# A branch on TensorE put behind four weight units, attention scores in pairs of heads, and key sums put ahead of row maxima

## The reference, cut to what matters

```python
def mla_mixer(...):
    ...
    q = rmsnorm(q, q_norm)                    # 8 heads of 128 + 64
    k = rmsnorm(k, k_norm)
    ...
    for blk in range(seq // Q_BLOCK):         # two blocks of 128 queries
        ...
        scores = jnp.einsum('bqhd,bkhd->bhqk', q[:, s0:end], k[:, :end]).astype(jnp.float32) * scale
        mask = jnp.arange(end)[None, :] <= (s0 + jnp.arange(Q_BLOCK))[:, None]
        p = jax.nn.softmax(jnp.where(mask, scores, neg), axis=-1).astype(v.dtype)
        outs.append(jnp.einsum('bhqk,bkhd->bqhd', p, v[:, :end]))

def moe_swiglu(h, router, w_gate, w_up, w_down):
    ...
    for e in range(N_EXPERTS):
        out = out + gates[:, e:e + 1] * swiglu(ht, w_gate[e], w_up[e], w_down[e])
```

## Time and profile before

| | us |
|---|---|
| median of three runs | 1259.41 |
| the profiled execution's own time | 1259.81 |
| its span, first to last instruction | 1257.9 |
| PE matmul busy | 1233.1 (98%) |
| DVE busy | 998.4 (79%) |
| ACT busy | 844.0 (67%) |

### The profile page before, as it was taken

One profiled execution on the slowest core, in us unless ns is written; L12 is line 12 of the kernel. 1 busy time (PEld: TensorE's weight loads), 2 busy tenths in 40 slices (PEclk: granted clock), 3 DMA queues, 4 the chain that ended last, 5 costly groups with the idle time before them and its releaser, 6 DMA issues.

```text
span 1257.9 us, 18129 instructions
## 1 busy us (share of the span) xinstructions
PE 1233.1 (98%) x5924; PEld 1015.4 (81%) x5924; DVE 998.4 (79%) x1397; ACT 844.0 (67%) x1218; POOL 40.0 (3%) x47
## 2 busy tenths in 40 slices
PE   7999999999999999999999999999999999999998
PEld 6888888888778788888888888888886877888887
DVE  5687555556876899999999999999999887765664
ACT  6566444446755788888888888888886686644443
POOL 0000000000100000000000000000100121000000
PEclk9999999999999999999999999999999999999999
DMA  9735545554233699999999999999997632455540
GB/s 365 293 126 225 196 173 191 177 196 168 70 134 133 246 379 372 383 344 367 371 396 366 362 374 365 392 350 364 370 421 281 245 146 101 168 184 185 184 150 34
DMA packets 48388, 325.41 MB, mean 259 GB/s; under 512 B 5512, under 2 KB 6672, under 8 KB 10192
## 3 DMA queue, kind: packets, MB, share of 16 engines
q1 hardware_dynamic: 44896, 316.59, 66.7%
q10 hardware_dynamic: 2752, 5.77, 1.2%
q0 software_dynamic: 688, 2.36, 0.5%
HBM read 318.93 MB, written 5.77 MB: 258 GB/s over the span
## 4 chain that ended last, share of the span: by engine, by line
PE 91%; DVE 4%; ACT 2%; issue 1%; DMA 1%; POOL 0%; SPq 0%; DVEq 0%; ACTq 0%
PE bank L434 26%; PE bank L436 26%; PE bank L435 25%; PE bank L1141 4%; PE bank L1142 2%; PE bank L498 2%; DVE wl L1834 1%; PE bank L848 1%; ACT wh L1202 1%; PE bank L703 1%; PE bank L470 1%; PE bank L1140 1%; DMA x<-x_dram 1%; PE bank L702 1%; DVE xt L1854 0%
## 5 line engine op out<-in xcount | busy, mean ns | idle before, releaser
L1834 DVE TENSOR_TENSOR wl<-raw,wh 128x1024 fp32r<-128x1024 f32 x598 | 712.7, 1219 | 171.0 <-ACT wh L1202 161.1
L1202 ACT ACTIVATE wh<-raw 128x1024 fp32r<-128x1024 f32 x598 | 630.3, 1058 | 266.6 <-PE bank L436 224.7
L434 PE MATMUL bank<-wh,xt 128*128 128x512 f32 (+2 forms) x1026 | 407.1, 397 | 5.7 <-DVE xt L1854 2.6
L436 PE MATMUL bank<-wh,xt 128*128 128x512 f32 (+2 forms) x1026 | 398.0, 388 | 0.0
L435 PE MATMUL bank<-wl,xt 128*128 128x512 f32 (+2 forms) x1026 | 397.3, 387 | 0.0
L434 PEld LDWEIGHTS bank<-wh,xt 128*128 128x128 f32 x1026 | 193.6, 189 | 44.7 <-DVE xt L1854 3.2
L436 PEld LDWEIGHTS bank<-wh,xt 128*128 128x128 f32 x1026 | 193.3, 188 | 40.3
L435 PEld LDWEIGHTS bank<-wl,xt 128*128 128x128 f32 x1026 | 194.0, 189 | 36.2
L434 PE MATMUL bank<-wh,hth 128*128 128x512 f32 x472 | 185.2, 392 | 0.1
L436 PE MATMUL bank<-wh,htl 128*128 128x512 f32 x472 | 184.1, 390 | 0.0
L435 PE MATMUL bank<-wl,hth 128*128 128x512 f32 x472 | 183.8, 389 | 0.0
(11 more groups left out here) (304 smaller groups left out, 809.2 us busy)
## 6 DMA issues: line engine op xcount, KB each, us to landing
raw<-weights_dram SPq DMA_DIRECT2D x298, 1024.0 KB, 6.5
expert_results<-wide ACTq DMA_DIRECT2D x7, 512.0 KB
x<-x_dram SPq DMA_DIRECT2D x2, 512.0 KB, 5.4
raw<-weights_dram SPq DMA_DIRECT2D x2, 512.0 KB, 7.4
wide<-bias_scratch ACTq DMA_DIRECT2D x8, 128.0 KB, 6.4
out_dram<-x SPq DMA_DIRECT2D x4, 256.0 KB, 2.0
fixed<-fixed_dram SPq DMA_DIRECT2D x1, 536.0 KB, 17.3
bias_scratch<-act ACTq DMA_DIRECT2D x2, 256.0 KB, 5.2
```

Source lines behind the costliest of these rows:

```text
L434: mm(o, lh, wh[:, wi, sl], start=start, stop=False)
L436: return mm(o, ll, wh[:, wi, sl], start=False, stop=stop)
L1202: A(wh[:, c % SPLIT, 0:n], raw[:, (c // 2) % RAW, (c % 2) * UNIT:(c % 2) * UNIT + n], ACT.Copy).then_inc(hi_done, 1)
L1834: V.tensor_tensor(wl[:, c % SPLIT, 0:n], raw[:, (c // 2) % RAW, (c % 2) * UNIT:(c % 2) * UNIT + n], f32(wh[:, c % SPLIT, 0:n]), ALU.subtra ...
```

## The change

- PE's branch for crowded experts becomes a function `crowd`, which runs behind the first four units of expert 0 instead of ahead of them. The load of the flag stays where it is. Inside the branch bank 1 takes the place of bank 0, on PE, ACT and DVE.
- Heads 0 and 1, and heads 4 and 5, get their scores by `scores_pair`: for each query block the 128-row products of both heads, then the 64-row products of both heads, which lie on different rows and in different banks. Heads 2, 3, 6 and 7 stay as they are.
- `k_sums(1)` goes ahead of `row_max(0)` on DVE.

```diff
             def ffn(tag, c0, nf, U, loops, width, nd, i0, f0=0, nt=NT, early=None, late=None, done=0, rows_ready=None,
-                    second=None, last_turn=None, first=False, half=0):
+                    second=None, last_turn=None, first=False, half=0, behind=None):
...
                     up(c0, i0, rows_ready)
                     if early:
                         early()
+                    if behind:
+                        behind()
                     up(c0 + ug, i0, None, bank[6:7], after={1: lambda: turn(0, fb)})
...
+            def scores_pair(h):
+
+                places = ((0, P), (P, 2 * P))
+                if h >= 2:
+                    pe.wait_ge(sem("head_nm"), h)
+                for qb, (a, n) in enumerate(places):
+                    for s in (h, h + 1):
+                        mm(bank[4 + s % 2][:, a:a + n], qnT[:, s, qb * P:(qb + 1) * P], knT[:, s, 0:n], start=True, stop=False)
+                    for s in (h, h + 1):
+                        r0 = (s % 2) * 64
+                        last = mm(bank[4 + s % 2][:, a:a + n], qrT[r0:r0 + 64, s // 2, qb * P:(qb + 1) * P],
+                                  krT[r0:r0 + 64, s // 2, 0:n], start=False, stop=True)
+                        if qb == 1:
+                            last.then_inc(sem("head_S"), 1)
...
-            scores(0)
-            scores(1)
+            scores_pair(0)
             pe.wait_ge(sem("v_c"), 2)
...
-            scores(4)
-            scores(5)
+            scores_pair(4)
             wo(0)
...
             crowded = pe.value_load(order[0:1, 9:10], min_val=0, max_val=1)
-            with pe.If(crowded > 0):
+
+            def crowd():
+
+                with pe.If(crowded > 0):
...
-            expert(0, 0, 2, first=True)
+            expert(0, 0, 2, first=True, behind=crowd)
...
             q_scales(0)
+            k_sums(1)
             row_max(0)
-            k_sums(1)
             row_max(1)
```

More of the change, by code:

```diff
@@ L886, in _ @@
             crowded = pe.value_load(order[0:1, 9:10], min_val=0, max_val=1)
-            with pe.If(crowded > 0):
[L888 to L909, removed]
-                            for n in range(2):
[L911 to L920, removed]
@@ new lines, in crowd @@
+            def crowd():
+                with pe.If(crowded > 0):
+                    pe.wait_ge(sem("moe_gl"), KD)
+                    pe.wait_ge(sem("order"), 2)
+                    passes = pe.value_load(order[0:1, 8:9], min_val=0, max_val=MORE)
+                    with pe.Fori(0, passes) as v:
+                        gather_rest(v)
+                        for t in range(NT):
+                            last = nc.tensor.transpose(bank[3][:, t * P:(t + 1) * P], osel[:, t, :], ident)
+                        last.then_inc(sem("o_selT"), 1)
+                        pe.wait_ge(sem("o_xt"), v * 2 + 2)
+                        for f in range(8):
+                            pe.wait_ge(sem("o_up"), v * 256 + 32 * (f + 1))
+                            for k in range(KD):
+                                last = mm(bank[1][:, :], oxt[:, k, :], opanel[:, k // 4, (k % 4) * WIDE:(k % 4 + 1) * WIDE],
+                                          start=(k == 0), stop=(k == KD - 1))
+                            last.then_inc(sem("o_gu"), 1)
+                            pe.wait_ge(sem("o_h"), v * 8 + f + 1)
+                            for j in range(2):
+                                last = nc.tensor.transpose(bank[2][:, j * P:(j + 1) * P], hbuf[:, 0, j * P:(j + 1) * P], ident)
+                            last.then_inc(sem("o_hT"), 1)
+                            pe.wait_ge(sem("o_hc"), v * 8 + f + 1)
+                            pe.wait_ge(sem("o_down"), v * 128 + 16 * (f + 1))
+                            for j in range(2):
+                                for n in range(2):
+                                    last = mm(bank[4 + n][:, :], oht[:, j, :],
+                                              opanel[:, 2, j * D + n * WIDE:j * D + (n + 1) * WIDE],
+                                              start=(f == 0 and j == 0), stop=(f == 7 and j == 1))
+                            last.then_inc(sem("o_d"), 1)
+                        pe.wait_ge(sem("o_y"), v * 2 + 2)
+                        for t in range(NT):
+                            for n in range(2):
+                                mm(bank[(2, 3, 1, 4)[2 * t + n]][:, :], oselt[:, t * P:(t + 1) * P],
+                                   oy[:, n * WIDE:(n + 1) * WIDE], start=True, stop=True).then_inc(sem("o_S"), 1)
+                        pe.wait_ge(sem("o_x"), v * 4 + 4)
@@ L1598, in _ @@
                         sc.wait_ge(sem("o_gu"), v * 8 + f + 1)
-                        A(ebuf[:, 0, 0:FG], bank[0][:, 0:FG], ACT.Tanh, scale=0.5).then_inc(sem("o_e"), 1)
+                        A(ebuf[:, 0, 0:FG], bank[1][:, 0:FG], ACT.Tanh, scale=0.5).then_inc(sem("o_e"), 1)
                         sc.wait_ge(sem("o_hT"), v * 8 + f + 1)
@@ L2494, in _ @@
                     for f in range(8):
-                        g, u, h = bank[0][:, 0:FG], bank[0][:, FG:2 * FG], hbuf[:, 0, 0:FG]
+                        g, u, h = bank[1][:, 0:FG], bank[1][:, FG:2 * FG], hbuf[:, 0, 0:FG]
                         dv.wait_ge(sem("o_e"), v * 8 + f + 1)
```

## The result

The changed kernel takes 1253.08 us in the median of five runs (1252.34 to 1255.49), beside 1259.86 for the kernel before: a ratio of 0.995 [0.9939, 0.9961], 6.8 us. Three more comparisons gave 0.9945 [0.9931, 0.9958], 0.9942 [0.9929, 0.9956] and 0.9952 [0.9939, 0.9965], or 6.6, 6.9 and 5.3 us. The profiled execution took 1252.34 us, with a span of 1250.4.

A forecast was written before the change was run, and what follows sets the result against it. TensorE (PE), holding 91% of the span, was taken to bound the kernel. Branch 2.1, first pair 0.85 and second pair 1.35 summed to 4.3 us, for a median of 1255.1 us, range 1253.6 to 1257.9.

The forecast's parts named there:

- gap ahead of the expert, removed: Before the first expert's unit 0: PE's idle time is its branch, and moving the branch saves 2.1 us.
- left over behind the fourth unit: After unit 3 of the first expert: PE's queue hides the moved 3.583 us branch except for 0 to 0.15 us.
- first pair, to the turning of head 0: Scores of heads 0 and 1: pairing saves 1.44 us, of which 0.85 arrives, between 0.4 and 1.4.
- second pair, to the turning of head 4: Scores of heads 4 and 5: pairing saves 1.44 us, of which 1.35 arrives, between 0.7 and 1.45.
- rival 1: First expert: ScalarE and VectorE are held behind their own branches; total gain 2.5 to 3.4 us, chance 0.12.
- rival 3: Paired scores: halves run one after the other, or weights come later; 0.9 us less gain, 1256.0 us, chance 0.10.
- Key sums ahead: VectorE before the first maximum: costs nothing under the later scores; without them, about a microsecond of delay.
- the cover: Behind unit 3: PE's queue runs 16 to 18 pairs ahead, covering 3.6 to 4.1 us of the branch.
- rival 2: Head of the expert gains nothing: VectorE release, or 2.1 us of branch open behind unit 3; 1257.2 us, chance 0.14.
- The step that failed: Whole kernel: gains are subtracted from the profiled execution of 1259.81 us, with the median taken 0.4 us lower.
- the addition of 0.7 for scatter: Range: 0.7 us added on either side because the runs shown spread 2.4 us, giving 1253.6 to 1257.9.
- rival 4: Moved branch: its target is fetched behind weight panels and the clock may fall; 3.9 us slower, 1263.3 us, chance 0.05.

The follow-up runs named there:

- the short body: Loop of passes left out of PE's branch for crowded experts: in the kernel before 1255.88 us (0.9972), in the changed kernel 1253.95 us (0.9945).
- the maximum first: Changed kernel with the first head's maximum put back ahead of the key sums on VectorE: 1255.51 us, 0.9963 of the kernel before.
- the shortened body: Changed kernel with the skipped branch body's eight panel steps written as one, a loop of six, and one: 1252.69 us, 0.9941 of the kernel before.
- the branch part alone: Kernel before with only the branch moved behind four units, scores and key sums as before: 1257.89 us, 0.9982 of the kernel before.
- the scores part alone: Kernel before with only the paired scores and the key sums first, the branch where it was: 1257.01 us, 0.9968 of the kernel before.
- the first pair and the branch: Changed kernel with heads 4 and 5 scored one after the other again: 1256.56 us, 0.997 of the kernel before.
- the shortened body and four pairs: Changed kernel with panel steps as one, a loop of six, and one, and heads 2, 3 and 6, 7 also paired: 1254.19 us, 0.9954 of before.
- the second experiment: Four kernels beside the kernel before (1259.60 us): changed with heads 4 and 5 unpaired, changed with maximum before key sums, before and changed without the branch's loop.
- the kernel before with more products: Kernel before with seven instead of three idle-filling products on TensorE ahead of the first gather: 1259.73 us, 0.9999 of the kernel before.
- A later arrival by 1.6 us: Changed kernel with ten idle-filling products ahead of the last turning of the first attention: 1256.12 us, 0.9967 of the kernel before.
- the four-pair kernel: Changed kernel with heads 2 and 3, and 6 and 7, scored in pairs too: 1253.67 us, 0.9953 of the kernel before.

## Why the prediction was wrong, although its terms held

**The terms.** At their own places, in traces:

| term | forecast us | measured us |
|---|---|---|
| gap ahead of the expert, removed | 2.1 | 2.26 |
| left over behind the fourth unit | 0 to 0.15 | 0.06 to 0.44 |
| first pair, to the turning of head 0 | 0.85 | 1.12 |
| second pair, to the turning of head 4 | 1.35 | 1.45 |
| sum | 4.3 | 4.4 to 4.8 |

The branch is what the gap was, as the earlier trace rows had it: shown by the short body. ACT and DVE moved with PE (0.61 and 0.79 us idle ahead of their first splits, for a forecast of 0.8 to 1.0), so rival 1 is out. The pairs take 2.65 and 2.73 us for a forecast of 2.60 to 2.63, so the halves run at the price of one, and rival 3 is out. Key sums ahead "cost nothing" because the later scores hide them; with the maximum first 0.71 us are gone, which the prediction had not priced (its microsecond is for key sums ahead without the pair's later scores). The one term that was a little off is the cover: "16 to 18 of them are 3.6 to 4.1 us", of which 0.15 go to the first load, and 3.40 were measured against a branch that varies from 3.44 to 3.86 us from trace to trace. So the gap of rival 2 behind the fourth unit is there, at a fifth of its price or less. The first pair came out 0.3 better than "between 0.4 and 1.4, I take 0.85", since nothing up to head 3 took back what it gave.

**The step that failed** is the first of the sum: "The sum is made against the profiled execution, 1259.81 us ... the median of the runs shown is 0.4 lower", and with it the addition of 0.7 for scatter at the end. It takes the stretches at 1.2 GHz of the kernel before as a fixed part of both kernels. They are not. Of 68 runs of the kernel before one has a mean granted clock of 0.999 or more, of 20 of the changed kernel 11. A line with one slope for both kernels, laid through these 88 runs against the mean clock, gives 0.65 us for each thousandth of clock and 5.5 us (standard error 0.2) between the kernels at equal clock; the mean clocks, 0.9967 and 0.9982, are worth another 1.0. Together that is the 6.5 us between the means. So of the 2.2 us that the forecast missed, 1.0 is clock and 0.1 to 0.5 the terms; the 0.7 to 1.1 that are left between 4.4 to 4.8 in the traces and 5.5 by the line are found in part only. The line counts a stretch at 1.2 GHz the same wherever it falls, and the traces don't. The kernel before and the changed kernel with the shortened body have two such stretches each in their traces, in router and gather and where the second attention begins. From the first score to the end they are 5.1 us apart (925.5 and 920.4), and 0.7 of that is the gather: the stretch costs 1.5 us where it begins with the gather, as in the kernel before, and 0.8 where it begins 2 us ahead of it, because there it first lengthens idle-filling products into a wait. That is one pair of traces, so the failed step accounts for 1.0 us by the line and for 1.7 perhaps; the rest stays open. The mean clock alone can't hold it: the 33 runs of the kernel before and the 5 of the changed one that both have 0.997 are 6.2 us apart in their means. The start of an execution scatters by more than what is left: in traces of the same changed kernel the first score comes at 331.36 and at 332.83 (above).

The prediction had the pieces. It quoted the clock of 0.69 in the gather, and in rival 4 priced a stretch at 1.2 GHz at 1.7 us, but only as a loss that the change might bring. That the same stretches are losses of the kernel before that the change might remove, since it takes out 2 us in which PE stands idle, was not asked. One such stretch taken off the low end, 1.7, would have put it at 1251.9 and the measured time inside.

**Why the clock is better** is settled in part only. Neither part alone gives it: the branch part alone has 0.999 or more in 1 of 11 runs, the scores part alone in 1 of 10, the first pair and the branch in 1 of 7, the kernel before with its gap closed by the short body in 0 of 9. But the whole change doesn't always keep it: with the maximum first it is 0 of 5, with the short body 1 of 5, with the shortened body and four pairs 1 of 5, beside 11 of 20 as it is. The short body takes one more wait out of PE's way, so less idle time alone doesn't make a better clock. The four kernels of the second experiment ran on one chip, and the changed kernel did not run on it, so that their clocks can't be told from the chip's; the kernel before had no lower clock there than elsewhere (0.9972 in the mean, 0.9964 to 0.9967 on the three others).

The 18 traces say where. A stretch at 1.2 GHz in router or gather stands in all 7 of kernels without the whole change and in 6 of the 11 with it (the one with the maximum first among them); one where the second attention begins in 3 of the 7 and 5 of the 11. So by this count, small as it is, the change makes the former rarer, the one that the prediction quoted as 0.69. Two further places are those that one part removes and the other leaves: behind the gap ahead of the expert, in two of the four traces with the gap (scores part alone; the kernel before with more products), and in the unpaired scores of heads 4 and 5, in one of six traces that have them (branch part alone). That the removal of idle time or of these places is the reason is argued, not shown. A later arrival by 1.6 us, at least, doesn't undo it.

## What to carry to other kernels

A gap of an engine is priced by its length and by what the clock does behind it: look for a granted clock below 1 in and behind each thin stretch that a change touches, and put one such stretch more and one less into the range. Where a branch that is not taken up costs microseconds, look at what it skips before moving it: here a body with the loop left out closed the same gap in place, while moving it costs whatever the queue doesn't cover. A shortened body that still does all of the work, 105 instructions, did not close it. Products on different row halves can be paired wherever the engine that runs them has no other wait next to them; where it has, the saving turns into that wait, as the four-pair kernel shows.

## What was not expected of the hardware

The time of PE's branch depends on what it skips, and at the lengths tried not in proportion: 238 and 354 ns over the few instructions of the short body, 3442 to 3863 ns over 105 or 185. The loops here that jump back over code that has run are cheap, at most 237 ns; these are the branches of the inner loop and of the one over pairs of experts, in the changed kernel by source line (min, median, max in ns):

```profile
L565 PEldq COMPARE_BRANCH  x23: 67/207/237, 163.9 to 936.2; - x23
...
L946 PEldq COMPARE_BRANCH  x3: 76/208/208, 608.9 to 886.5; - x3
```

And two executions of the same code can differ in the clock at the same place: the gather of the changed kernel took 3.9 us at 2.4 GHz in one trace and 5.4 with a stretch at 1.2 GHz in another, with the same 0.77 us of idle time ahead of it.
